# Three 256-column matmuls per weight block in place of one of 512 and one of 256, two PSUM banks a group, and groups evicted straight from PSUM

## The reference

```
h = rmsnorm(x); z = h @ w_in                      # conv_in, latents
u = silu(layernorm(causal_conv31(a * sigmoid(g))))
q = rmsnorm(q_lat) @ w_uq; kv = rmsnorm(kv_lat) @ w_ukv
x += rmsnorm(concat(rmsnorm(u), rmsnorm(attn(q, kv))) @ w_out)
x += rmsnorm((silu(hf @ w_gate) * (hf @ w_up)) @ w_down)
...
x += (gated delta rule | moba attention of rmsnorm(x) @ w_in_2) @ w_out_2
x += cross_attention(x, mem) @ w_xo_2
x += (silu(causal_conv3(h @ w_gate_2) + b) * (h @ w_up_2)) @ w_down_2
return rmsnorm(x)
```

## Time and profile before

| what | us |
|---|---|
| median of 3 runs | 2845.27 (2844.9 to 2856.12) |
| span of the profiled execution, first to last instruction | 2835.2 |
| median less span (the profiled execution's own time outside its span is not given) | 10.1 |
| TensorE busy in the span (matmuls) | 2592.4, 91% |
| TensorE weight loads busy | 2236.5, 79% |
| VectorE busy | 1761.2, 62% |
| ScalarE busy | 1321.3, 47% |
| mean granted TensorE clock | 0.947 |

### The profile page before, as it was taken

How to read it: one execution, slowest core, us unless ns; L and a number is a source line. 1 busy time by engine, 2 the same in 40 slices (tenths; PEclk the granted TensorE clock), 3 DMA queues, 4 the chain that set the end, 5 groups by cost and what they waited for, 6 DMA issues and landing times.

```text
span 2835.2 us, 38341 instructions
## 1 busy us (share of the span) xinstructions
PE 2592.4 (91%) x14428; PEld 2236.5 (79%) x14428; DVE 1761.2 (62%) x2413; ACT 1321.3 (47%) x1836; POOL 15.6 (1%) x34
## 2 busy tenths in 40 slices
PE   6979687999999999979989877899799999999997
PEld 5868375888888888868878657788688888888886
DVE  5889467665666644465685435366787666775454
ACT  5445455544444443444444432345564554544342
POOL 0000000000000000000010000000000000000000
PEclk9989688999999999989989958999999999999998
DMA  6543044565555555535555300044255655555453
GB/s 206 178 120 119 0 134 133 164 192 185 187 190 192 191 186 178 187 105 193 180 191 192 111 0 1 35 164 165 98 164 191 192 187 186 189 192 193 173 190 112
DMA packets 235580, 435.90 MB, mean 154 GB/s; under 512 B 14040, under 2 KB 32488, under 8 KB 235360
## 3 DMA queue, kind: packets, MB, share of 16 engines
q1 hardware_dynamic: 232368, 424.02, 46.2%
q0 software_dynamic: 1968, 6.44, 0.6%
q10 hardware_dynamic: 1152, 4.19, 0.4%
HBM read 432.51 MB, written 3.68 MB: 154 GB/s over the span
## 4 chain that ended last, share of the span: by engine, by line
PE 82%; DVE 12%; ACT 3%; issue 1%; DMA 1%; DVEq 0%; SPq 0%; ACTq 0%
PE ps L629 48%; PE ps L632 25%; DVE w_lo L403 3%; DVE ssq L768 1%; DVE ar L926 1%; PE ps L1183 1%; DVE x L736 1%; PE ps L786 1%; PE ps L950 1%; PE ps L1163 1%; PE ps L1531 1%; PE ps L1528 1%; DVE ar L481 1%; PE ps L1010 1%; PE ps L1522 1%
## 5 line engine op out<-in xcount | busy, mean ns | idle before, releaser
L629 PE MATMUL ps<-x,w_hi 128*128 128x512 f32 x5064 | 1792.7, 398 | 89.4 <-DVE x L736 60.4
L403 DVE TENSOR_TENSOR w_lo<-w_raw,w_hi 128x1024 fp32r<-128x1024 f32 (+3 forms) x820 | 986.1, 1208 | 798.1 <-ACT w_hi L397 792.6
L632 PE MATMUL ps<-x,w_lo 128*128 128x256 f32 x5064 | 1427.3, 282 | 0.0
L397 ACT ACTIVATE w_hi<-w_raw 128x1024 fp32r<-128x1024 f32 (+3 forms) x820 | 853.3, 1046 | 1037.6 <-PE ps L632 1008.8
L629 PEld LDWEIGHTS ps<-x,w_hi 128*128 128x128 f32 x5064 | 961.3, 190 | 318.3 <-issue 73.9
L632 PEld LDWEIGHTS ps<-x,w_lo 128*128 128x128 f32 x5064 | 968.7, 191 | 0.4
L629 PE MATMUL ps<-h,w_hi 128*128 128x512 f32 x1408 | 494.8, 396 | 4.7 <-DVE w_lo L403 4.7
L632 PE MATMUL ps<-h,w_lo 128*128 128x256 f32 x1408 | 395.5, 281 | 0.0
L629 PEld LDWEIGHTS ps<-h,w_hi 128*128 128x128 f32 x1408 | 264.7, 188 | 67.6 <-issue 4.7
L632 PEld LDWEIGHTS ps<-h,w_lo 128*128 128x128 f32 x1408 | 266.8, 190 | 0.0
L417 ACT ACTIVATE half<-ps 128x256 f32<-128x256 f32 x380 | 142.3, 381 | 79.9 <-PE ps L632 76.8
(11 more groups left out here) (254 smaller groups left out, 1404.3 us busy)
## 6 DMA issues: line engine op xcount, KB each, us to landing
w_raw<-in_w_gate SPq DMA_DIRECT2D x88, 1024.0 KB, 5.2
w_raw<-in_w_up SPq DMA_DIRECT2D x88, 1024.0 KB, 5.2
w_raw<-in_w_down SPq DMA_DIRECT2D x88, 1024.0 KB, 5.0
w_raw<-in_w_in SPq DMA_DIRECT2D x80, 1024.0 KB, 5.1
w_raw<-in_w_out SPq DMA_DIRECT2D x32, 1024.0 KB, 5.1
w_raw<-in_w_xkv SPq DMA_DIRECT2D x8, 1024.0 KB, 5.0
w_raw<-in_w_uq SPq DMA_DIRECT2D x18, 256.0 KB, 3.6
w_raw<-in_w_ukv SPq DMA_DIRECT2D x16, 256.0 KB, 3.8
```

The source lines that it names most:

```text
L397: nc.scalar.activation(w_hi[:, u % HIS, 0:ks.stop - ks.start, cs], w_raw[:, slot(g, j), ks, cs], ACT.Copy)\
L403: nc.vector.tensor_tensor(w_lo[:, slot(g, j), ks, cs], w_raw[:, slot(g, j), ks, cs], w_hi[:, u % HIS, 0:ks.stop - ks.start, cs].bitcast(F3 ...
L629: nc.tensor.matmul(bank, w_hi[:, u % HIS, k - ks.start, c0:c0 + P], both.rearrange("p a n -> p (a n)"), start=(n == 0 and k == 0), stop=False)
L632: ins = nc.tensor.matmul(bank[:, T:2 * T], w_lo[:, slot(g, j), k, c0:c0 + P], hi, start=False, stop=(final and k == ks.stop - 1))
```

## The change

A block is now three matmuls of 256 columns that all add to the same 256 columns of PSUM. Two blocks share a bank, so a group takes two banks; groups alternate between banks 0-1 and 2-3, over the borders of the products too, and banks 4 to 7 hold only statistics, attention and the like. The whole sum stands in PSUM, so `half`, L417 and the additions of L481 go: a group is evicted by two instructions of 512 columns, one a bank: VectorE multiplies by `rs_x` straight from PSUM (after: L493), or adds PSUM to `xt` (`add`), or ScalarE copies (`sum`). The waits on `bank_free` (one a bank) and `group_out` give way to one semaphore `evicted`, of which a group waits for the group two before it. The wait for all earlier banks at the head of `multiply`, and the wait for `st_done`, are gone.

```diff
-            return x2[:, k], x2[:, k, 0, :]
+            return x2[:, k, 0, :], x2[:, k, 1, :]
...
-                gr["t"], gr["e"], gr["n"] = at, bank, k
+                gr["t"], gr["n"], gr["banks"] = at, k, 2 * ((g.q0 + k) % 2)
...
+        def pair(gr, b):
+            M = len(gr["at"])
+            bank = ps[:, gr["banks"] + b, :].rearrange("p (c t) -> p c t", c=2)
+            if M == 1:
+                h = slice(b * P, (b + 1) * P)
+                return 0, 1, h, ps[:, gr["banks"], h].unsqueeze(1)
+            n = min(2, M - 2 * b)
+            return 2 * b, n, slice(0, T), bank[:, 0:n, :]
...
+        def evicted_by(g, i, gr):
+            return AHEAD_E + 2 * (g.q0 + gr["n"]) + i * (2 * len(g.groups)) + 2
...
         def evict_act(act, g, i, gr):
-            for m in range(M):
-                act.wait_ge(products, last + m + 1)
-                nc.scalar.activation(half[:, m, :], ps[:, gr["banks"] + m, 0:T], ACT.Copy).then_inc(half_out, 1)
+            if gr["kind"] == "sum":
+                where, base_c, step = gr["out"]
+                for b in range(2):
+                    c, n, h, bank = pair(gr, b)
+                    group_ready(act, g, i, gr, b)
+                    nc.scalar.activation(chunk(where, base_c + c, step, i, n), bank, ACT.Copy).then_inc(evicted, 1)
...
         def evict_dve(dve, g, i, gr):
-            for m in range(M):
-                dve.wait_ge(half_out, e + m + 1)
-                nc.vector.tensor_tensor(dst(m), half[:, m, :], ps[:, gr["banks"] + m, T:2 * T], ALU.add)\
-                    .then_inc(bank_free, 1)
...
-                nc.vector.tensor_tensor(whole, whole, bc(g.scale, M), ALU.mult)\
-                    .then_inc(group_out, 1)
+            for b in range(2):
+                c, n, h, bank = pair(gr, b)
+                group_ready(dve, g, i, gr, b)
+                v = bc(scale, n)
+                nc.vector.tensor_tensor(dst(c, n)[:, :, h], bank, v[:, :, h], ALU.mult).then_inc(evicted, 1)
...
         def multiply(pe, g, *stats, between=None):
-            pe.wait_ge(bank_free, AHEAD_B + g.e0 - (0 if stats else kept))
...
-                    if stats and first_turn(i) and gr["banks"] == 4 and n == 0 and u > FIRST:
-                        pe.wait_ge(st_done, STATS[stats[-1]][0] + 1)
+                    if n == 0:
+                        pe.wait_ge(evicted, evicted_by(g, i, gr) - 4)
...
-                            nc.tensor.matmul(bank, w_hi[:, u % HIS, k - ks.start, c0:c0 + P],
-                                             both.rearrange("p a n -> p (a n)"),
-                                             start=(n == 0 and k == 0), stop=False)
-                            ins = nc.tensor.matmul(bank[:, T:2 * T], w_lo[:, slot(g, j), k, c0:c0 + P], hi,
-                                                   start=False, stop=(final and k == ks.stop - 1))
+                            nc.tensor.matmul(out_m, w_h, x_h, start=(n == 0 and k == 0 and m % 2 == 0), stop=False)
+                            nc.tensor.matmul(out_m, w_h, x_l, start=False, stop=False)
+                            ins = nc.tensor.matmul(out_m, w_lo[:, slot(g, j), k, c0:c0 + P], x_h, start=False,
+                                                   stop=(final and k == ks.stop - 1 and (m % 2 == 1 or m == M - 1)))
```

More of the change, by code:

```diff
@@ L290, in build @@
                         for b in (0, 4)], x2c, rs_x),
-            Gemm("w_out_2", 2, [group(turned(w_loop(A["w_out_2"], b * P, 2 * W)), 4, banks=b, out=(xt, 0 + b, 8), kind="add")
+            Gemm("w_out_2", 2, [group(turned(w_loop(A["w_out_2"], b * P, 2 * W)), 4, out=(xt, 0 + b, 8), kind="add")
                         for b in (0, 4)], lambda k: x2c((k + 8) % DC)),
-            Gemm("xkv", 1, [group(w_cols(A["w_xkv_2"], b * P, W), 4, banks=b, out=(ar, XK + b, 0)) for b in (0, 4)], x2c, rs_x),
+            Gemm("xkv", 1, [group(w_cols(A["w_xkv_2"], b * P, W), 4, out=(ar, XK + b, 0)) for b in (0, 4)], x2c, rs_x),
@@ L450, in evict_dve @@
             kind = gr["kind"]
+            if kind == "sum":
+                yield
+                yield
+                reduce_group(dve, g, i, gr)
+                return
             if kind == "add":
                 _, base_c, step = gr["out"]
-                xc = lambda m: chunk(xt, base_c + m, step, i)
-                for m in range(M):
-                    dve.wait_ge(half_out, e + m + 1)
-                    nc.vector.tensor_tensor(xc(m), xc(m), ps[:, gr["banks"] + m, T:2 * T], ALU.add)\
-                        .then_inc(add_half, 1)
-                a0 = g.a0 + gr["e"] + i * g.banks
-                for m in range(M):
-                    dve.wait_ge(add_half, a0 + m + 1)
-                    nc.vector.tensor_tensor(xc(m), xc(m), half[:, m, :], ALU.add).then_inc(bank_free, 1)
+                for b in range(2):
+                    c, n, h, bank = pair(gr, b)
+                    group_ready(dve, g, i, gr, b)
+                    x = chunk(xt, base_c + c, step, i, n)
+                    nc.vector.tensor_tensor(x, x, bank, ALU.add).then_inc(evicted, 1)
                 if g.name in STREAM_STAT:
@@ L703, in build @@
         G["down_2"].needs = lambda k: (hid_lo, FC + k)
-        adds = 0
-        for g in GEMMS:
-            g.a0 = adds
-            adds += g.turns * g.banks if g.groups[0]["kind"] == "add" else 0
         def prep_act(act, name, src, gain, ready=None, square=None, after=None):
@@ L876, in rope_pe @@
         def rope_pe(pe):
-            pe.wait_ge(bank_free, AHEAD_B + G["w_out"].e0)
+            pe.wait_ge(evicted, AHEAD_E + 2 * G["w_out"].q0)
             for c in range(4):
@@ L1886, in _ @@
             multiply(pe, G["z_ba"])
-            pe.wait_ge(bank_free, AHEAD_B + G["z_ba"].e0 + 8)
             rel_pe(pe)
```

138 lines of the change are left out of this document (55 added, 83 removed).

## The result

The changed kernel takes **2883.66 us** (median of 4 runs, 2880.03 to 2886.1), the kernel before in the same comparison 2850.69 us (4 runs, 2844.9 to 2856.19). The ratio is **1.0105**, 95% interval 1.0076 to 1.0134: slower, by about one per cent. The prediction of 2844 us, with a range of 2824 to 2868, did not hold; it gave a slower kernel 0.18.

The account below looks back on a forecast made before the run. TensorE was taken to bound the kernel (82% of the chain). Blocks +21.0, evictions -10.2, freed waits -7.5 and -4.3 gave -1.0 us on a 2835.2 us span; with 10.1 us around it, 2844 us, range 2824 to 2868.

Parts of the forecast that it names:

- The block: Three 256-column matmuls at 0.1167 us each, 0.350 us a block, 0.0033 more than before; +21 us over 6472 blocks.
- Rival B: TensorE cannot be fed a load and a matmul per 0.1167 us; slower by 17.5 us at 0.1176; chance 0.08.
- The bounds: Block cost on TensorE between 0.345 us (-10.8 us in sum) and 0.52 us (+1122 us).
- the likeliest case: Blocks 19 to 26 us dearer, seams worth 12 to 30 us: 2834 to 2859 us; chance 0.72.
- The base: Time around the 2835.2 us span of the kernel before, taken as 10.1 us by the median and unchanged.
- Evictions: Two evicting instructions a group take 1.3 us, 1.35 us less on VectorE; with the ends of products, -10.2 us.
- the plain seams: Six borders between products where TensorE waits behind an eviction on VectorE; 1.35 us less each, 8.1 us.
- Rival A: Seams give next to nothing, as other VectorE work or ScalarE replaces the eviction; 2861 to 2866 us; chance 0.08.
- The two waits: Waits freed from `latents` through `uq` and `ukv` (-7.5 us) and from `z_ba` to `qkv_b` (-4.3 us).
- no wait above 3 us: Sign to look for: at the head of `uq`, TensorE no longer waits longer than 3 us.
- Rival D: Blocks get cheaper, each of the three matmuls at 0.115 us or less; 2812 us; chance 0.10.
- Rival C: Weight loads go one after another at 0.187 us each; 4210 us; chance 0.02.

Follow-up runs that it names:

- e1: Kernel before, with only its 512-column matmul cut into two of 256 columns, into the two halves of the same bank; 2902.22 us against 2846.63, ratio 1.019.
- e4: Changed kernel without the second matmul of each block (high weights by low activations); 2222.79 us.
- e3: Changed kernel, the second matmul of each block with 64 of its 128 weight columns; 2823.29 us.
- e8: Changed kernel, all three matmuls of a block on 128 of the 256 tokens, except where an accumulation starts; 3353.25 us.
- e9: Changed kernel, every matmul with 64 of the 128 weight columns, except where an accumulation starts and stops; 2779.47 us.
- e2: Changed kernel, the second matmul of each block on 128 of the 256 tokens; 2834.91 us.
- e7: Changed kernel unaltered, measured again; 2889.79 us, ratio 1.0123 to the kernel before.
- e5: Changed kernel with the old waits back at the heads of products with statistics and `qkv_b`, and for `st_done`; 2883.11 us, ratio 1.0118 to the kernel before.
- e6: Kernel before with only the waits at `uq` and `qkv_b` relaxed, by other banks and group order; 2839.89 us, ratio 0.9967.
- e11: Kernel before, its 512-column matmul with 64 of the 128 weight columns, except where an accumulation starts; 2821.16 us against 2851.1.
- e10: Kernel before, its 256-column matmul on 128 of the 256 tokens; 2792.66 us against 2851.1.

## Why the prediction was wrong

**The block: the step that failed.** "I take 0.1167 us for each of the three" priced a block at 0.350; it is 0.360. The term of +21 us measured +69. The 0.1167 was the distance from the start of a 256-column matmul to that of a 512-column one in a pair; it does not carry over to a stream in which every matmul has 256 columns and a whole load. What came in its place is a step of 0.120, in e1 and e4 too. The cause by e3, e8 and e9: at the full clock the load of 128 weight columns takes 0.112 us when only 128 columns stream beside it, hardly less than 256 columns with 0.1135 when the load is halved, and with both whole a step is 0.120. One of the two loads of a pair had 512 columns for a cover; now each has 256. e1 shows that the cut in two is enough for the dearer block, and e9 that with halved loads three matmuls take 0.341, less than a pair with whole ones.

An even split of the excess, which looks like a rule, is not one. A pair of 0.3467 is 0.320 of columns and twice 0.0133 on top, and 0.320 + 3 x 0.0133 is 0.360; but the longer pair of 0.3533 would give 0.370 that way, and e2, with 640 columns in three matmuls, 0.307 where 0.353 was measured. That it meets the 0.360 is luck.

**Rival B came true, just past its point.** It was to decide at 0.1176 us a matmul and named the reason, that every load would have the short shadow. It had 0.08, since the earlier trace rows were read as proof that TensorE can be fed: 0.1125 us for 128 columns and a load. In the light of e8 that row says something else: 128 columns need 0.053, so the 0.1125 was the load's own price. The evidence was in the rows, read for the wrong quantity. The rule of the Trainium skill that was weighed there ("Perfetto Trace Analysis", "Identifying the Most-Contended Engine", to judge TensorE by the busy share of its loads, beside its share of the peak arithmetic) pointed at the right resource. This trace agrees with it as a warning: 352.69 of 400 us before, 400 of 400 after. The prediction took the loads of L629 alone for it, half of the window; those of both lines filled 88%. But the share does not tell which resource binds, as e9 shows 400 of 400 too, with nearly all loads halved. The price of 0.561 us a block, which the prediction worked out from the length of the load records, was wrong by far.

On the same question the Trainium skill, "TensorE: Matmul & The Clock Gate", section "Back-to-back issue gap", says that in a stream of loads and matmuls both set the spacing, and gives N / 2.4 + 2.5 ns for an isolated matmul, by which an estimate for 256 columns is 109 ns. The runs here agree with the first and measure 120.0 ns in the stream; no run has an isolated one.

**The bounds.** The upper bound that was worked out for a block (0.52 us) and the lower (0.345) did hold the value, but the range was drawn from the likeliest case, 19 to 26 us for the blocks, narrower than the reading could bear.

**The base.** What lies around the span is 1.8 us, not 10.1: the profiled execution was one of the short ones, with the shorter pair in `ffn` and `ffn_2`. At 0.0133 us more in every one of 6472 blocks the change would cost 86 us; it cost 69 in the profiles, in part since some products had the longer pair before. The medians differ by less, 33.0 us, which would fit if more products have it in most executions; that was not profiled.

**Evictions.** 1.28 us for two (1.3 foreseen). Without the seam behind `qkv_b`, the plain seams and the ends gave 9.6 us, of which 8.9 were foreseen: 2.5 at `latents`, 1.1 each at `xkv` and `xq`, 0.4 ahead of the cross attention, 1.5 at `ffn_2`, 2.6 at the end, and 0.5 net at `w_out` and `down`. The 4.9 us after `qkv_b` are not settled: that stretch, with attention and gated delta rule, lasts 236.1 us in the changed kernel, 237.8 in e7 and 228.2 in e5, which do not differ in it (241.0 and 241.8 before and in e6). Rival A (the seams give nothing) falls by the profiles; no run measures the seams alone but for e6's two.

**The two waits.** `uq` started 6.2 us earlier (5.1 foreseen, 3 to 10), though much of it turns into the wait for `q`'s statistic; from the end of `latents` to the end of `uq` 5.5 us stay. `ukv`'s end gave 2.7 (2.4 foreseen), `qkv_b` 3.9 (4.3). That "no wait above 3 us" would stand at the head of `uq` was right, that the matmul after `kv`'s sum follows at once too; the new 9.44 us stand ahead of that sum.

**Not foreseen**: the "issue" stalls, 6.7 us. The account by terms, against the prediction's: blocks 48 us more than the +21, stalls 7, seams 5.4 the other way, the start 0.6. That is the whole difference between -1.0 and +49.1.

**Rival D** (cheaper blocks) falls with e1 and e4: with whole loads throughout, a matmul of 256 columns took 0.120 in every steady stretch, not 0.115 or less. **Rival C** (0.561 us a block) falls as well.

## What to carry to other kernels

The distance from one start to the next inside a mixed repeat is not the price of that instruction in a stream of its own kind; and where a term decides between faster and slower, one edit of the kernel before that makes it alone, as e1 does, prices it. Here a 128-column load costs about as much as 256 columns (0.112 and 0.1135 us), so a matmul that streams 256 leaves the load no slack. Cutting one of 512 columns in two, with the weights loaded again, cost 13 ns a time against the shorter pair and 7 against the longer, though no column was added. Ask of every short reference stretch which of its two resources it measures, and take a freed wait without the rest of a change where the two can be parted (e6).

## What the runs showed of the hardware that was not expected

**Less work, a lower clock.** e8 streams half the columns with as many matmuls and loads, and takes 3353 us, 470 more than the changed kernel. Its mean granted clock is 0.757 (0.952 there). From 2200 to 2300 us TensorE is busy throughout and the clock is 0.50, 1.2 GHz; from 700 to 1000, with the same pattern, it is 1.00. In `down` it falls about 1 us after the loop's turn, at which TensorE had waited 2.27 us for VectorE, and stays at 0.50 from 1242 to 1460 us, in which TensorE is busy for 217.57 of 218. At the lower level its timeline has

```profile
2250.47 0.41 PE L619 MATMUL ps<-x,w_hi 128*128 128x128 f32 x1
2250.68 0.41 PE L620 MATMUL ps<-x,w_hi 128*128 128x128 f32 x1
2250.89 0.41 PE L621 MATMUL ps<-x,w_lo 128*128 128x128 f32 x1
```

steps of 0.21 us for 128 columns, as long as the changed kernel needs for 256 at that level: the load takes time by the same clock, and at 1.2 GHz a load and 256 columns overlap with nothing lost. Why the clock stays low no run isolates.

**Two lengths of a pair.** What sets a pair to 0.3467 or 0.3533, and changes it at a loop's turn, stays open. e11, with half the `w_hi` load, has 0.340 and 0.3467, and e10, with 128 columns fewer, 0.340 in every product, so both load and columns have a part in it.

**A stall in a long loop.** Some 5 us of "issue" at the turn of `down_2` stand in the changed kernel, e7, e2, e3, e8 and e9, whose loop body has three matmuls a block, but not in e1 and e5, which have three as well. In `down`, whose body is as long (352 blocks), all eight of these profiles have such a stall within eight blocks of the turn, of 1.1 us in the changed kernel, 3.0 in e5 and 3.8 in e1. None of the profiles with two matmuls a block (before, e4, e6, e10, e11) has one of 1 us or more there. So it goes with the long body. That the instructions were not there in time is the likely reading; it was not tested.
